# First attention of a two-layer block: the softmax weights are turned unscaled, and the scale is applied to the weighed output

## Chip, cores and metric

The kernel runs on one core of a Trainium2 chip. The metric is the device time of one execution in microseconds (us), median over several runs.

## What is computed

Two transformer-like blocks run one after the other on 512 tokens of width 1024, all in fp32. The first has, side by side, a neighbourhood attention with 8 heads of 64 and a two-directional state-space layer (SSD) with 8 heads of 64; their outputs are joined, go through `w_out`, and a gated feed-forward follows. The second block is a windowed attention and another feed-forward. The change lies in the first attention alone. Cut to its core, the reference says, for each grid row of 64 queries:

```python
s_loc = einsum("bwhd,brwkhd->bhwrk", q_r, k_win) * scale + bias     # 8 x 16 window
s_ctx = einsum("bwhd,bchd->bhwc", q_r, k_ctx) * scale               # 256 context keys
p = softmax(concatenate([s_loc, s_ctx], -1))
out = einsum(p_loc, v_win) + einsum(p_ctx, v_ctx)
```

## The kernel before

Weights stream in as 92 blocks of 128 x 2048. The large products take three passes in a rounded fp32 type: every operand x is held as a high part and a low part (x minus the high part), and TensorE (PE) adds high·high, high·low and low·high (`chunk_products`, L274). So every weight block and every activation needs a high part (a copy by ScalarE, ACT) and a low part (a subtraction by VectorE, DVE, or GpSimd, POOL). Semaphores are set by hand, and each engine runs its own program in the order in which it is written.

The first attention works on 16 groups (`NG = 16`), four query windows for each of four pairs of heads. A group G has two units, u = 2G and 2G + 1, one for each head of the pair, and a unit is 128 queries by 512 keys. The engines walk over turns. In turn G:

- PE (`attention1_pe`): `scores(G)` (L508, four products of 128 x 256 in all), `turn(G - 2)` for both units (L522, four 128 x 128 transposes each, into banks 1 and 2), `weigh(G - 3)` (L536, values times turned weights, two heads side by side on 64 output rows each, into bank 7 or 3). Scores have four banks.
- DVE (`attention1_dve`): `top` for both units (L601 and L603: bias added, and the row's extreme found), `inverse(G - 1)` (L610: reciprocal of the two row sums), `out_low(G - 4)` (L615: low half of the output, read from the bank). In turns 7, 9, 11 and 13 also a quarter of the low half of weight block 13 (L634).
- ACT (`attention1_act`): `exp` for both units (L562, it also sums the rows), `copy(G - 1)` for both units (L572, turned weights from the bank to SBUF), `out_high(G - 2)` (L578). The high half of weight block 13 (L258) stands between turns 3 and 4.
- POOL (`attention1_pool`): for each unit, the unscaled weights times the reciprocal of their row sum (L648), ahead of the turn; and after units 9, 13, 17 and 21 a quarter of the low half of weight block 12 (L656).

Turn 0 and turn 1 lie between the last projection products (tiles 22 and 23 of the input projection). Right behind the attention stands the SSD. Its first part is a chain of ten steps: POOL makes scaled inputs (L941), PE multiplies them (L968), DVE adds the product to the carried state (L1104 for the first two, then L1099 and L1102). POOL's step n waits for PE's step n - 2, PE's step n for DVE's step n - 2. Then PE makes masked sums (`sums`, L977 and L985), ACT the decay factors (L1069, L1073), and so on.

Of the kernel before, what the change touches and what calls it, by code (L numbers as in the profile page):

```python
# [6 lines left out]
ALU = mybir.AluOpType  # L7
# [90 lines left out]
def build(nc, T):  # L98

    es = ExitStack()  # L100
    with es:
# [98 lines left out]
        at1 = {n: sem(f"att1_{n}") for n in ("scores", "top", "nmax", "probs", "rinv", "norm", "ptr", "pt", "pv", "ohi", "olo")}  # L200
# [292 lines left out]
        prob1, pt1 = [A(at, 512) for at in A_PROB], [A(at, 4, 256) for at in A_PT]  # L493

        def attention1_pe(pe, turns):
# [29 lines left out]
            def weigh(G):  # L525
                j, t = G // 4, G % 4
                pe.wait_ge(s["pt"], 2 * G + 2)
                if G >= 2:
                    pe.wait_ge(s["olo"], G - 1)
                elif G == 1:  # L530
                    pe.wait_ge(tile_free, 24)
                for kb in range(4):
                    for odd in range(2):
                        head, half = slice(128 * j + 64 * odd, 128 * j + 64 * odd + 64), slice(128 * odd, 128 * odd + 128)
                        v = vkey[:, 2 * t + kb, head] if kb < 2 else vctx[:, kb - 2, head]
                        last = nc.tensor.matmul(ps[WEIGH1[G % 2]][64 * odd:64 * odd + 64, 0:128], v, pt1[G % 2][:, kb, half],  # L536
                                                start=kb == 0, stop=kb == 3)
                last.then_inc(s["pv"], 1)
# [10 lines left out]
        def out1(G):  # L549
            j, t = G // 4, G % 4  # L550
            hi, lo = (h[:, j:j + 1, :].rearrange("p a (r t c) -> p (a t) r c", r=ROWS, t=4)[:, t] for h in (h_hi, h_lo))
            return hi, lo, ps[WEIGH1[G % 2]][:, 0:128].rearrange("p (r c) -> p r c", r=ROWS)

        def attention1_act(act, turns):
# [20 lines left out]
            def out_high(G):  # L575
                act.wait_ge(s["pv"], G + 1)
                hi, lo, src = out1(G)
                nc.scalar.activation(hi, src, ACT.Copy).then_inc(s["ohi"], 1)  # L578

            for G in turns:  # L580
# [9 lines left out]
                if G >= 2:  # L590
                    out_high(G - 2)

        def attention1_dve(dve, turns):
# [18 lines left out]
            def out_low(G):  # L612
                dve.wait_ge(s["ohi"], G + 1)
                hi, lo, src = out1(G)
                nc.vector.tensor_tensor(lo, src, hi, ALU.subtract).then_inc(s["olo"], 1)  # L615

            for G in turns:
                if G == 2:
                    inverse(1)
# [3 lines left out]
                if G == 1:  # L623
                    inverse(0)
                if 3 <= G < NG + 1:
                    inverse(G - 1)
                if G in (7, 9, 11, 13):
                    q = (G - 7) // 2
                    if q == 0:
                        dve.wait_ge(hi_done, B_OUT + 2)  # L630
                    if q == 3:
                        dve.wait_ge(lo_done, B_OUT + 1)
                    part = slice(q * 512, q * 512 + 512)
                    last = nc.vector.tensor_tensor(w_lo[1][:, part], w_raw[1][:, part], w_hi[1][:, part], ALU.subtract)  # L634
                    if q == 3:
                        last.then_inc(lo_done, 1)
                if G >= 4:
                    out_low(G - 4)
# [5 lines left out]
        def attention1_pool(pool):  # L644
            s = at1
            for u in range(2 * NG):
                pool.wait_ge(s["rinv"], u // 2 + 1)
                nc.gpsimd.tensor_scalar(prob1[u % 4], prob1[u % 4], row_inv[:, u % 16:u % 16 + 1], 1.0,  # L648
                                        ALU.mult, ALU.mult).then_inc(s["norm"], 1)
                if u in (9, 13, 17, 21):  # L650
                    q = (u - 9) // 4
                    if q == 0:
                        pool.wait_ge(hi_done, B_OUT + 1)
                        pool.wait_ge(half_used, 2 * (B_OUT - 1))
                    part = slice(q * 512, q * 512 + 512)
                    last = nc.gpsimd.tensor_tensor(w_lo[0][:, part], w_raw[0][:, part], w_hi[0][:, part], ALU.subtract)  # L656
                    if q == 3:
                        last.then_inc(lo_done, 1)

# [431 lines left out]
        def ssd_dve(dve, link):  # L1091
            for n in range(10):
                d, k, c = n % 2, n // 2, ORDER[n % 2][n // 2]
                new = state0[:, d, :] if k == 0 else hin[:, 4 * d + AFTER[d][k], :]
                if k:
# [3 lines left out]
                    link(nc.vector.tensor_tensor(heads(new), heads(old), dec, ALU.mult))  # L1099
                dve.wait_ge(sd["st"], n + 1)  # L1100
# [575 lines left out]
        def _(act):  # L1676
# [110 lines left out]
            attention1_act(act, range(4, NG + 2))  # L1787
# [699 lines left out]
```

## Time and profile before

| | |
|---|---|
| median of 3 runs | 1347.22 us (1346.64 to 1348.71) |
| the profiled execution | 1348.49 us, of which the profile's span is 1346.7 us |
| PE matmul busy | 1292.5 us (96%) |
| DVE, ACT, POOL busy | 550.3, 569.1 and 594.8 us |
| granted PE clock, mean | 0.988 |
| the attention, from turn 2's first turned unit to the end of the last weighing | 245 to 297.6 us |

The profile's line numbers are those of the kernel before. In a timeline, one line is a run of equal instructions: its start, its length, and in brackets how long the engine had been idle and what ended that. An fp32 product takes two PE instructions, so `scores` counts 8, the transposes of a group 8, and `weigh` 16.

### The profile page before, as it was taken

Reading aid. Unit: us, or ns where it says so; the run is one execution under the profiler, and the core shown is the slowest. Engines: PE = TensorE matmul, PEld = TensorE weight load, DVE = VectorE, ACT = ScalarE, POOL = GpSimd, SP = SyncE. Lnnn points to the kernel's source line nnn. Section 1 sums busy time; section 2 is a strip of 40 time slices with the busy share of each in tenths; the row PEclk is TensorE's granted clock in tenths of the full one; section 3 lists DMA queues with packets and bytes.
Section 4 is the critical chain, followed back from the end, with each engine's and each line's share of the span. In section 5 each row is a group of like instructions: output and inputs, shape, how many; then the busy total and the mean of one; then the engine's idle time right before and its main releaser. Section 6 shows DMA issues by size and latency. Waiting matters only on the chain.

```text
span 1346.7 us, 17535 instructions
## 1 busy us (share of the span) xinstructions
PE 1292.5 (96%) x6464; PEld 1037.7 (77%) x6464; DVE 550.3 (41%) x1080; ACT 569.1 (42%) x938; POOL 594.8 (44%) x494
## 2 busy tenths in 40 slices
PE   8999999898989999999999899999899999999998
PEld 1788888676877888888888778667688888888886
DVE  2577652678436444443542362783520000001123
ACT  3712454777335333222323364785452323223232
POOL 0335232367235444444665642455224444445561
PEclk9899999999989999999999999999999999999999
DMA  9417547050233555554422312111202233222221
GB/s 393 177 75 272 186 167 146 1 188 1 68 152 130 208 195 196 198 195 156 156 94 94 141 63 94 56 29 62 92 32 94 96 102 106 101 93 94 94 93 63
DMA packets 27401, 166.76 MB, mean 124 GB/s; under 512 B 2976, under 2 KB 5280, under 8 KB 8656
## 3 DMA queue, kind: packets, MB, share of 16 engines
q1 hardware_dynamic: 25328, 151.31, 32.2%
q10 hardware_dynamic: 2016, 14.68, 2.9%
q8 instruction: 37, 0.61, 0.2%
q14 instruction: 20, 0.16, 0.0%
HBM read 163.85 MB, written 6.32 MB: 126 GB/s over the span
## 4 chain that ended last, share of the span: by engine, by line
PE 83%; DVE 7%; ACT 4%; DMA 3%; POOL 1%; issue 1%; SPq 0%; DVEq 0%; ACTq 0%
PE bank L274 54%; PE bank L333 12%; PE bank L310 6%; DMA ada_ring<-ada_dram 2%; DVE ada_ring L2005 1%; PE bank L1346 1%; PE bank L1318 1%; DMA w_raw<-w_dram 1%; PE bank L522 1%; PE bank L713 1%; DVE arena L2070 1%; PE bank L536 1%; PE bank L508 1%; POOL arena L941 1%; PE bank L702 1%
## 5 line engine op out<-in xcount | busy, mean ns | idle before, releaser
L267 POOL TENSOR_TENSOR w_lo<-w_raw,w_hi 128x512 fp32r<-128x512 f32 x336 | 457.8, 1393 | 615.8 <-ACT w_hi L258 615.8
L274 PE MATMUL bank<-h_hi,w_hi 128*128 128x512 f32 x1120 | 442.7, 395 | 9.6 <-DVE h_lo L449 6.6
L274 PE MATMUL bank<-h_lo,w_hi 128*128 128x512 f32 x1120 | 438.8, 392 | 0.0
L274 PE MATMUL bank<-h_hi,w_lo 128*128 128x512 f32 x1120 | 438.6, 392 | 0.0
L258 ACT ACTIVATE w_hi<-w_raw 128x2048 fp32r<-128x2048 f32 x88 | 168.6, 1916 | 306.5 <-PE bank L274 187.8
L274 PEld LDWEIGHTS bank<-h_hi,w_hi 128*128 128x128 f32 x1120 | 212.3, 190 | 57.0 <-issue 6.3
L274 PEld LDWEIGHTS bank<-h_hi,w_lo 128*128 128x128 f32 x1120 | 212.0, 189 | 44.6
L274 PEld LDWEIGHTS bank<-h_lo,w_hi 128*128 128x128 f32 x1120 | 212.4, 190 | 42.6
L2342 DVE TENSOR_TENSOR arena<-arena,bank 128x512 f32 (+1 forms) x22 | 15.1, 688 | 210.2 <-PE bank L274 210.2
L2198 DVE TENSOR_TENSOR h_lo<-arena,h_hi 128x1024 fp32r<-128x1024 f32 x22 | 32.4, 1486 | 135.1 <-ACT h_hi L1822 123.6
L2024 DVE SCALAR_TENSOR_TENSOR arena<-bank,params,arena 128x511 f32<-128x511 f32 (+1 forms) x36 | 25.4, 705 | 130.0 <-ACT arena L1797 109.7
L333 PE MATMUL bank<-w_hi,h_hi 128*128 128x512 f32 x176 | 68.7, 390 | 0.0
L333 PE MATMUL bank<-w_lo,h_hi 128*128 128x512 f32 x176 | 68.5, 389 | 0.0
L333 PE MATMUL bank<-w_hi,h_lo 128*128 128x512 f32 x176 | 68.5, 389 | 0.0
L2015 DVE CUSTOM_DVE_ANT_0 ada_ring<-ada_ring,arena 128x1024 f32<-128x1024 f32 x48 | 62.3, 1334 | 0.0
L2005 DVE CUSTOM_DVE_ANT_0 ada_ring<-ada_ring,arena,params 128x1024 f32<-128x1024 f32 x32 | 48.1, 1545 | 10.6 <-DMA ada_ring<-ada_dram 10.4
L898 POOL TENSOR_SCALAR arena<-arena,small 128x256 f32<-128x256 f32 (+1 forms) x64 | 33.2, 532 | 36.4 <-DVE small L839 36.4
L1797 ACT ACTIVATE arena<-bank,params 128x512 f32<-128x512 f32 x22 | 17.1, 779 | 70.4 <-PE bank L274 70.4
L310 PE MATMUL bank<-h_hi,w_hi 128*128 128x512 f32 x112 | 43.7, 390 | 0.0
L310 PE MATMUL bank<-h_hi,w_lo 128*128 128x512 f32 x112 | 43.6, 389 | 0.0
L310 PE MATMUL bank<-h_lo,w_hi 128*128 128x512 f32 x112 | 43.6, 389 | 0.0
L1346 PE MATMUL bank<-arena_rounded,w_hi 128*128 128x256 f32 x224 | 40.4, 282 | 2.7 <-DVE arena L2026 1.8
(274 smaller groups left out, 1714.4 us busy)
## 6 DMA issues: line engine op xcount, KB each, us to landing
w_raw<-w_dram SPq DMA_DIRECT2D x92, 1024.0 KB, 4.8
ada_ring<-ada_dram SPq DMA_DIRECT2D x30, 1024.0 KB, 4.8
ada_ring<-ada_dram ACTq DMA_DIRECT2D x14, 1024.0 KB, 4.9
arena<-ada_dram SPq DMA_DIRECT2D x4, 1024.0 KB, 10.7
arena<-x_dram SPq DMA_DIRECT2D x2, 2048.0 KB, 11.5
bias_copies<-bias_rows SPq DMA_DIRECT2D x1, 4096.0 KB, 17.4
arena<-bias_copies SPq DMA_DIRECT2D x4, 768.0 KB, 5.8
ada_ring<-rpb_dram SPq DMA_DIRECT2D x16, 128.0 KB, 9.4
```

The costliest lines, as they stand in the source:

```text
L258: nc.scalar.activation(w_hi[b % 2][:], w_raw[b % 2][:], ACT.Copy).then_inc(hi_done, 1)
L267: last = nc.gpsimd.tensor_tensor(w_lo[b % 2][:, part], w_raw[b % 2][:, part], w_hi[b % 2][:, part], ALU.subtract)
L274: last = nc.tensor.matmul(bank[:, :], w[:, ft, k, :], x[:, k, :], start=k == first and m == 0, stop=k == final and m == 2)
L310: last = nc.tensor.matmul(ps[f][:, :], w[:, k, f, :], x[:, 2 * gslot + k, :], start=bank_free is not None and k == 0 and m == 0, stop=False)
L333: last = nc.tensor.matmul(ps[2 * t + h][:, :], x[:, slot + k, part], w[n][:, k, cols], start=start and m == 0, stop=stop and m == 2)
L898: nc.gpsimd.tensor_scalar(prob2[:, u % 8, 0:w], prob2[:, u % 8, 0:w], row_inv[:, u % 16:u % 16 + 1], 1.0, ALU.mult, ALU.mult).then_inc(s[" ...
L1346: last = nc.tensor.matmul(ps[4 + n % 2][:, 0:CTX], w[:, n % 2, k, :], x[:, k, :], start=k == 0 and m == 0, stop=k == DC - 1 and m == 2)
L1797: nc.scalar.activation(buf, bank[:, :], ACT.Identity, bias=fconv[:, 3, bass.ds(j, 1)], scale=fconv[:, 1, bass.ds(j, 1)]).then_inc(tap_done, 1)
L2005: last = nc.vector.tensor_tensor_reduce(out=src, in0=src, in1=row1, scale=1.0, scalar=par_("adab")[:, 16 + at:17 + at], op0=ALU.mult, op1= ...
L2015: last = nc.vector.tensor_tensor_reduce(out=src, in0=src, in1=row2, scale=1.0, scalar=0.0, op0=ALU.mult, op1=ALU.add, accum_out=dots[:, 2 ...
L2024: link(nc.vector.scalar_tensor_tensor(out=buf[:, 1:n], in0=src[:, 0:n - 1], scalar=w[:, 0, m], in1=buf[:, 1:n], op0=ALU.mult, op1=ALU.add))
L2198: nc.vector.tensor_tensor(h_lo[:, slot:slot + 2, :], HID[:, chunk, :], h_hi[:, slot:slot + 2, :], ALU.subtract)\
```

## The change

The weights are no longer scaled ahead of the turn. `turn` waits for the exponentials (`probs`) alone, and POOL's 32 scalings (L648) and their semaphore go. In their place `weigh(G)` first makes two products on PE: the column of reciprocals of each unit, repeated over 64 stationary columns, times the identity, which puts each query's reciprocal into columns 128 to 256 of the output bank, beside the weighed output. DVE (`out_scale`) copies these 128 columns to SBUF, and multiplies the output of the bank by them into one of two SBUF buffers. ACT's `out_high` reads that buffer, two turns later than before, and POOL now makes the low half (`out1_low`), from SBUF. DVE's `inverse` moves by a turn (`inverse(G - 2)` in turn G). POOL takes the low halves of both weight blocks 12 and 13, a quarter ahead of each `out1_low` of groups 1 to 8; DVE's L634 goes. The last two `out1_low`, of groups 14 and 15, stand in the SSD's first POOL loop, ahead of its step 4.

```diff
             def turn(G, odd):
                 u = 2 * G + odd
-                pe.wait_ge(s["norm"], u + 1)
+                pe.wait_ge(s["probs"], u + 1)
...
                 pe.wait_ge(s["pt"], 2 * G + 2)
                 if G >= 2:
-                    pe.wait_ge(s["olo"], G - 1)
+                    pe.wait_ge(s["scaled"], G - 1)
...
+                pe.wait_ge(s["rinv"], G + 1)
+                for odd in range(2):
+                    col = (2 * G + odd) % 16
+                    nc.tensor.matmul(ps[WEIGH1[G % 2]][64 * odd:64 * odd + 64, 128:256], row_inv[:, col:col + 1].to_broadcast([P, 64]), ident,
+                                     start=True, stop=True)
...
+        def out1_low(G):
+            nc.gpsimd.wait_ge(at1["ohi"], G + 1)
+            hi, lo, src = out1(G)
+            nc.gpsimd.tensor_tensor(lo, src, hi, ALU.subtract).then_inc(at1["olo"], 1)
...
             def out_high(G):
-                act.wait_ge(s["pv"], G + 1)
+                act.wait_ge(s["scaled"], G + 1)
...
-                if G >= 2:
-                    out_high(G - 2)
+                if G >= 4:
+                    out_high(G - 4)
...
+            def out_scale(G):
+                dve.wait_ge(s["pv"], G + 1)
+                nc.vector.tensor_copy(inv_spread[:, G % 2, :], ps[WEIGH1[G % 2]][:, 128:256]).then_inc(s["spread"], 1)
+                if G >= 2:
+                    dve.wait_ge(s["olo"], G - 1)
+                dve.wait_ge(s["spread"], G + 1)
+                nc.vector.tensor_tensor(out_scaled[G % 2], ps[WEIGH1[G % 2]][:, 0:128], inv_spread[:, G % 2, :], ALU.mult).then_inc(s["scaled"], 1)
...
         def attention1_pool(pool):
...
-                nc.gpsimd.tensor_scalar(prob1[u % 4], prob1[u % 4], row_inv[:, u % 16:u % 16 + 1], 1.0,
-                                        ALU.mult, ALU.mult).then_inc(s["norm"], 1)
...
+            for G in range(NG - 2):
+                if 1 <= G < 9:
+                    b, q = (G - 1) // 4, (G - 1) % 4
...
+                    last = nc.gpsimd.tensor_tensor(w_lo[b][:, part], w_raw[b][:, part], w_hi[b][:, part], ALU.subtract)
...
+                out1_low(G)
...
             for n in range(10):
                 d, c = n % 2, ORDER[n % 2][n // 2]
+                if n == 4:
+                    for G in (NG - 2, NG - 1):
+                                out1_low(G)
```

In the change the lines have other numbers: the transposes are L523, the spreading products L536, the weighing L542, `out1_low` L563, and the SSD's first POOL loop L942. PE's program at the end of the attention stood so before (turns 15 to 18, then the SSD's L968):

```order
L508 MATMUL bank<-arena 128x256 x4
L522 MATMUL bank<-constants,arena 128x128 x8
L536 MATMUL bank<-arena 64x128 x8
L522 MATMUL bank<-constants,arena 128x128 x8
L536 MATMUL bank<-arena 64x128 x8
L522 MATMUL bank<-constants,arena 128x128 x8
L536 MATMUL bank<-arena 64x128 x16
L968 MATMUL bank<-arena 128x256 x20
```

and now (turns 16 to 18):

```order
L523 MATMUL bank<-constants,arena 128x128 x8
L536 MATMUL bank<-constants,small 64x128 x2
L542 MATMUL bank<-arena 64x128 x8
L523 MATMUL bank<-constants,arena 128x128 x8
L536 MATMUL bank<-constants,small 64x128 x2
L542 MATMUL bank<-arena 64x128 x8
L536 MATMUL bank<-constants,small 64x128 x2
L542 MATMUL bank<-arena 64x128 x8
L969 MATMUL bank<-arena 128x256 x20
```

Each weighing has two more products ahead of it, and nothing else moved on PE. POOL's program from the attention into the SSD stood so before:

```order
L656 TENSOR_TENSOR w_lo<-w_raw,w_hi 128x512
L648 TENSOR_SCALAR arena<-arena,small 128x512 [waits att1_rinv] x10
L941 TENSOR_TENSOR arena<-arena,small 128x512 [waits ssd_wend]
L941 TENSOR_TENSOR arena<-arena,small 128x512
L941 TENSOR_TENSOR arena<-arena,small 128x512 [waits ssd_st] x8
```

and now (the `out1_low` of groups 12 to 15 and the ten L942; `small` and `w_dt` are the two buffers of the scaled output):

```order
L563 TENSOR_TENSOR h_lo<-small,h_hi 128x8x16 [waits att1_ohi]
L563 TENSOR_TENSOR h_lo<-w_dt,h_hi 128x8x16 [waits att1_ohi]
L942 TENSOR_TENSOR arena<-arena,small 128x512 [waits ssd_wend]
L942 TENSOR_TENSOR arena<-arena,small 128x512
L942 TENSOR_TENSOR arena<-arena,small 128x512 [waits ssd_st] x2
L563 TENSOR_TENSOR h_lo<-small,h_hi 128x8x16 [waits att1_ohi]
L563 TENSOR_TENSOR h_lo<-w_dt,h_hi 128x8x16 [waits att1_ohi]
L942 TENSOR_TENSOR arena<-arena,small 128x512 [waits ssd_st] x6
```

POOL's first SSD step now stands behind a wait for ACT's high half of group 13, and two low halves stand between its steps 3 and 4.

## Rows read from the trace of the kernel before

**Rows 1.** The page: busy time of PE, and the chain that ended last
```profile
PE 1292.5 (96%) x6464; PEld 1037.7 (77%) x6464; DVE 550.3 (41%) x1080; ACT 569.1 (42%) x938; POOL 594.8 (44%) x494
...
PE 83%; DVE 7%; ACT 4%; DMA 3%; POOL 1%; issue 1%; SPq 0%; DVEq 0%; ACTq 0%
```

**Rows 2.** Busy time of each engine in 245 to 298 us
```profile
245.00:298.00 53.00, 49.33 (x490) 36.54 (x491) 36.99 (x126) 42.78 (x108) 30.75 (x38) 1.00 0.28 97
```

**Rows 3.** Waits in 245 to 298 us: total us, times, longest
```profile
PE bank L522 <- POOL arena L648: 4.5, 4, 1.8
```

**Rows 4.** Chain that ended last: start, us, what
```profile
262.41 1.06 PE bank L508 x8
263.47 1.02 PE bank L522 x8
264.49 1.02 PE bank L536 x16
...
301.22 8.44 POOL arena L941 x6
...
311.55 2.19 ACT ada_ring L1069 x8
```

**Rows 5.** Timeline of turns 7, 8, 9 and 15 to the SSD: start us, us, engine, what
```profile
262.34 1.13 PE L508 MATMUL bank<-arena 64*128 64x256 f32 x8
...
265.45 1.13 PE L508 MATMUL bank<-arena 64*128 64x256 f32 x8
...
266.60 1.32 PE L522 MATMUL bank<-constants,arena 128*128 128x128 f32 x8
...
268.87 1.13 PE L508 MATMUL bank<-arena 64*128 64x256 f32 x8
...
288.48 1.14 PE L508 MATMUL bank<-arena 64*128 64x256 f32 x8
...
292.39 1.32 PE L522 MATMUL bank<-constants,arena 128*128 128x128 f32 x8 [0.72 <-POOL arena L648]
...
297.58 1.99 PE L968 MATMUL bank<-arena 128*128 128x256 f32 x8
```

**Rows 6.** Nearest rows for the new operations: groups by shape, one timeline line, one line's durations
```profile
L898 POOL TENSOR_SCALAR arena<-arena,small 128x256 f32<-128x256 f32 x32 | 14.9, 478 | 15.4 <-DVE small L839 15.4
...
355.10 1.05 PE L1055 MATMUL bank<-constants,small 128*128 128x128 f32 x8
...
L941 POOL TENSOR_TENSOR arena<-arena,small x10: 1037/1483/2026, 294.9 to 308.2; 128x512 f32<-128x512 f32 x10
...
L2105 DVE COPY y_squares<-small x2: 220/223/226, 202.8 to 203.0; 128x128 f32<-128x128 f32 x2
```

**Rows 7.** Timeline of turns 2 to 6, where the loop fills
```profile
247.95 0.69 DVE L2080 TENSOR_TENSOR arena<-arena 128x512 f32<-128x512 f32 x1
...
251.84 1.13 PE L508 MATMUL bank<-arena 64*128 64x256 f32 x8
...
255.78 1.90 ACT L258 ACTIVATE w_hi<-w_raw 128x2048 fp32r<-128x2048 f32 x1
...
259.07 1.13 PE L508 MATMUL bank<-arena 64*128 64x256 f32 x8 [0.40 <-ACT arena L562]
```

**Rows 8.** Timeline of the last turns and the SSD's first steps, in order of time
```profile
294.66 1.09 PE L522 MATMUL bank<-constants,arena 128*128 128x128 f32 x8
...
294.95 3.03 POOL L941 TENSOR_TENSOR arena<-arena,small 128x512 f32<-128x512 f32 x2
...
295.30 1.77 DVE L641 TENSOR_TENSOR arena_rounded<-y_squares,constants 128x1024 fp32r<-128x1024 f32 x1
295.36 1.09 ACT L572 ACTIVATE arena<-bank 128x512 f32<-128x512 f32 x2 [0.30 <-PE bank L522]
...
296.83 0.28 ACT L578 ACTIVATE h_hi<-bank 128x128 fp32r<-128x128 f32 x1 [0.38 <-PE bank L536]
...
298.80 2.16 POOL L941 TENSOR_TENSOR arena<-arena,small 128x512 f32<-128x512 f32 x2 [0.83 <-PE bank L968]
```

More of the change, by code:

```diff
@@ L199, in build @@
             "add_left", "add_right", "x_left", "x_right", "x_bias", "x_root", "x_inv", "xn_left", "xn_right"))
-        at1 = {n: sem(f"att1_{n}") for n in ("scores", "top", "nmax", "probs", "rinv", "norm", "ptr", "pt", "pv", "ohi", "olo")}
+        at1 = {n: sem(f"att1_{n}") for n in ("scores", "top", "nmax", "probs", "rinv", "ptr", "pt", "pv", "spread", "scaled", "ohi", "olo")}
         at2 = {n: sem(f"att2_{n}") for n in ("scores", "nmax", "probs", "sinkin", "sinke", "rinv", "norm",
@@ L493, in build @@
         prob1, pt1 = [A(at, 512) for at in A_PROB], [A(at, 4, 256) for at in A_PT]
+        out_scaled, inv_spread = [small[:, 384:512], wdt[:, :]], A(A_STATE + 512, 2, 128)
         def attention1_pe(pe, turns):
@@ L551, in out1 @@
             hi, lo = (h[:, j:j + 1, :].rearrange("p a (r t c) -> p (a t) r c", r=ROWS, t=4)[:, t] for h in (h_hi, h_lo))
-            return hi, lo, ps[WEIGH1[G % 2]][:, 0:128].rearrange("p (r c) -> p r c", r=ROWS)
+            return hi, lo, out_scaled[G % 2].rearrange("p (r c) -> p r c", r=ROWS)
+        def out1_low(G):
+            nc.gpsimd.wait_ge(at1["ohi"], G + 1)
+            hi, lo, src = out1(G)
+            nc.gpsimd.tensor_tensor(lo, src, hi, ALU.subtract).then_inc(at1["olo"], 1)
         def attention1_act(act, turns):
@@ L610, in inverse @@
                 nc.vector.reciprocal(row_inv[:, two], row_sum[:, two]).then_inc(s["rinv"], 1)
[L612 to L615, printed above, removed]
+            def out_scale(G):
[5 more added lines that the diff above has]
+                nc.vector.tensor_tensor(out_scaled[G % 2], ps[WEIGH1[G % 2]][:, 0:128], inv_spread[:, G % 2, :], ALU.mult).then_inc(s["scaled"], 1)
             for G in turns:
-                if G == 2:
-                    inverse(1)
                 if G < NG:
@@ L622, in attention1_dve @@
                     top(G, 1)
[L623 to L636, printed above, removed]
+                if 2 <= G < NG + 2:
+                    inverse(G - 2)
                 if G >= 4:
-                    out_low(G - 4)
+                    out_scale(G - 4)
                 if G in (NG + 1, NG + 2):
@@ L644, in attention1_pool @@
         def attention1_pool(pool):
-            s = at1
-            for u in range(2 * NG):
-                pool.wait_ge(s["rinv"], u // 2 + 1)
-                nc.gpsimd.tensor_scalar(prob1[u % 4], prob1[u % 4], row_inv[:, u % 16:u % 16 + 1], 1.0,
-                                        ALU.mult, ALU.mult).then_inc(s["norm"], 1)
-                if u in (9, 13, 17, 21):
-                    q = (u - 9) // 4
+            for G in range(NG - 2):
+                if 1 <= G < 9:
+                    b, q = (G - 1) // 4, (G - 1) % 4
                     if q == 0:
-                        pool.wait_ge(hi_done, B_OUT + 1)
+                        pool.wait_ge(hi_done, B_OUT + 1 + b)
+                    if G == 1:
                         pool.wait_ge(half_used, 2 * (B_OUT - 1))
                     part = slice(q * 512, q * 512 + 512)
-                    last = nc.gpsimd.tensor_tensor(w_lo[0][:, part], w_raw[0][:, part], w_hi[0][:, part], ALU.subtract)
+                    last = nc.gpsimd.tensor_tensor(w_lo[b][:, part], w_raw[b][:, part], w_hi[b][:, part], ALU.subtract)
                     if q == 3:
                         last.then_inc(lo_done, 1)
+                out1_low(G)
         NG = 16
@@ L1099, in ssd_dve @@
                     link(nc.vector.tensor_tensor(heads(new), heads(old), dec, ALU.mult))
+                if n == 1:
+                    dve.wait_ge(at1["scaled"], NG)
                 dve.wait_ge(sd["st"], n + 1)
@@ L1786, in _ @@
             high(act, B_OUT + 1)
-            attention1_act(act, range(4, NG + 2))
+            attention1_act(act, range(4, NG + 4))
             ssd_act(act)
```

## Prediction

> **What bounds the kernel now.** I read the page first. PE is busy for 96% of the span, and the chain that ended last is PE for 83% [rows 1]: time is lost or won where PE waits or gets more work. So the place of the change has to be looked at for PE alone. From 245 to 298 us PE is busy for 49.3 of 53 us, ACT for 42.8, DVE for 37.0 and POOL for 30.8 [rows 2]. The waits of that stretch say what is missing: PE's transposes waited 4.5 us in four longer waits for POOL's scaling [rows 3]. That wait is what the change takes away. What is it worth, and what do the added products cost?
>
> The chain gives the length of PE's parts when nothing holds them: scores 1.06 us, the eight transposes 1.02, the weighing's 16 instructions 1.02 [rows 4], so a turn takes 3.10. The timeline agrees for turn 7, whose scores start at 262.34 and those of turn 8 at 265.45. Turn 8 takes 3.42, to 268.87, since its transposes are spread over 1.32 instead of some 1.06: POOL was late by 0.3 us [rows 5]. This pair repeats: the scores of turn 15 start at 288.48, eight turns after turn 7, so a turn takes 3.27 on average. The loop is thus bound by PE's own work, with 0.16 us of waiting a turn.
>
> **The added products.** Each weighing gets two fp32 products of 64 output rows by 128 columns, four PE instructions of the form that L536 has (there the two heads go side by side on 64 output rows each, and here too). 16 of these take 1.02 us [rows 4], so one takes 0.064 and four take 0.26. From above: if the pair did not overlap, each instruction would cost what a full-width one of the same kind costs, a repeated column times the identity, 1.05 / 8 = 0.131 [rows 6], so 0.52 for four. From below: nothing, if they slip into time that PE loses anyway between parts. I take 0.26, since L536 has their shape and their neighbours. A turn then takes 3.10 + 0.26 = 3.36, against 3.27 before: **the products cost 0.1 us a turn more than the removed wait gives.**
>
> **PE, turn by turn.** The first turned units may now start at once behind the scores of turn 2, but this gives nothing: copying them out waits for DVE's L2080, which ends at 248.6 [rows 7] and does not move, and DVE's next four row maxima, 0.87 us each, follow. I get the scores of turn 4 at 251.8, as before (251.84). From there nothing holds PE. Turn 4 gains what its transposes waited for POOL. In turn 6 the scores waited for ACT, 0.40 us, because the high half of weight block 13, 1.9 us, stood ahead of the exponentials [rows 7]. ACT now starts it some 0.8 us earlier, since no high half of an output, with its wait for the weighing, is in front of it any more, and ends the exponentials by 258.3. PE wants them at 251.8 + 2 x 3.36 = 258.5, so this wait goes too. The scores of turn 15 start at 251.8 + 11 x 3.36 = 288.8, where 288.48 was. Turn 15 ends at 292.1. Turns 16 and 17 have no scores: 2.30 each, without the 0.72 us that turn 16 waited for POOL at 292.39 [rows 5]. They end at 296.7, and the last weighing, 1.28, at 298.0. Before, the SSD's first product started at 297.58 [rows 5]. Net so far: **+0.4 us.**
>
> **The other engines in the loop.** ACT has the same work. Its high halves read SBUF two turns later, when they are ready, so it no longer waits for PE there: 2.7 us of work in 3.36. DVE loses L615 and its quarter subtractions, and gets a copy of 128 columns, some 0.22 us [rows 6], and a multiplication like L615: with 37.0 of 53 us busy, or 2.3 of 3.3 a turn [rows 2], it stays under 2.7 a turn. POOL has 1.3 us for a quarter and one small subtraction a turn. `scaled` and `rinv`, for which PE's weighing now waits, are made in the DVE turn before. I cost all of this at nothing. The cover is 0.6 us a turn on DVE and ACT; if it were gone, each 0.1 us of it would cost 1.4 us. The SP queue's loads of blocks 14 and 15 wait for the low halves; these are done no later than before.
>
> **POOL's small subtraction.** The trace has none of 128 columns. It reads 2 x 128 elements, as the scaling of 256 columns does, 0.48 us [rows 6]. Below: a quarter of the fastest L941 of 512 columns, 1.04 / 4 = 0.26. Above: 0.48 times the slowdown of a typical L941 against the fastest, 1.48 / 1.04 [rows 6], 0.68. I take 0.48. The Trainium skill (GPSIMD Engine Reference, section 3.1) has 4497 ns for this operation on 2048 columns, against 2293 on the vector engine, and so speaks against moving it; an estimate from it in proportion is 0.28, and the sum below would be +1.4 instead of +2.0.
>
> **The end, where POOL is on the path.** Behind the attention the chain is POOL's: L941 back to back for 8.44 us from 301.22 [rows 4]. Before, POOL made the first two steps from 294.95, 3.03 us, while PE was still weighing; step 2 then waited for PE and started at 298.80 [rows 8]. Now POOL may start step 0 only behind the low half of group 13, and this behind ACT's high half. The last transposes start at 294.4; the copies start 0.70 later (295.36 behind 294.66), take 1.1 to 296.2, then come two high halves, 0.28 each [rows 8], to 296.75, and the low half with its semaphore, 0.55: POOL starts step 0 at 297.3 instead of 294.95. Two steps take 3.03 beside DVE's L641 and 2.16 without [rows 8]; L641 is beside about half of them, so 2.7. The fast and the slow price differ, I think, because DVE's L641 and L1099 read two SBUF operands. The Trainium skill (GPSIMD Engine Reference, section 8) says that POOL shares its SBUF interfaces with such DVE instructions; by it the slow price would hold for just as long as L641 runs, and if that were all of both steps the sum would be +2.3. Step 2 starts at 300.0, 1.2 later than before. Steps 2 and 3 took 2.42 before, of which 0.27 a wait for PE; now 2.2, and then two low halves, 0.96, stand in front of step 4: 303.2 instead of 301.22. **So +2.0 us, which contains the 0.4.** Steps 4 to 9, the sums and ACT's decay factors from 311.55 on [rows 4] are one chain behind it and move by the same 2.0; later PE is full, nothing gives it back.
>
> **The sum.** The profiled execution would go from 1348.5 to 1350.5. It is 1.3 above the median of the runs; against the median, 1347.2 + 2.0 = **1349.2 us**. A measurement of this kernel tells about 0.2% from no change, 2.7 us, so this is within "same", near its edge. The forecast's own range, with the bounds of the three low halves on the path (-0.7 to +0.6) and of the two POOL steps (-0.5 to +0.3), is 1348.0 to 1350.2.
>
> **The rivals.**
> 1. *The two spreading products do not overlap* (0.52 instead of 0.26 in 15 weighings, from turn 4 on). PE's own work decides, so all of it counts: +3.9 more, 1353.1, slower. For it: only an order of one head's two instructions, then the other's, and a stationary operand that is one column repeated, which no row has at 64 columns. Against it: L536 has the same order and costs 0.064. It turns the sign of the verdict as soon as four instructions take over 0.30 us. Chance 0.15.
> 2. *POOL stays longer on the path*: POOL beside DVE is slowed in all its steps, or an `out1_low` is as dear as 0.68 and the loop's last ones queue up. Up to 1351.3. Chance 0.12.
> 3. *The products are hidden*: they cost next to nothing, a turn takes 3.10, and -3.9 stands against the +2.0: 1345.3. This is the other sign. The point from which it decides is 0.13 us for four instructions. For it: PE's instructions overlap at their ends, a 128-column one lasts 0.27 in the trace and takes 0.13. Against it: the chain already counts the overlapped time. Chance 0.10.
> 4. *The removed wait comes back as another*: PE waits for the exponentials or for `scaled`. By the times above the exponentials are over 2 us early, and `scaled` 1.8. Then 1350 to 1353, or in turns with luck no loss; with all that I don't see, chance 0.08.
>
> **How the numbers follow.** The forecast has 0.55: 0.42 within 0.2% and 0.13 above. Rival 1 is slower (0.15), rival 2 mostly (0.08 of 0.12), rival 3 is 0.07 same and 0.03 faster, the rest 0.04 faster, 0.02 and 0.02. That makes faster 0.07, same 0.55, slower 0.38. The range reaches to rivals 3 and 1: 1345.3 to 1353.1; what lies outside is part of the rest.
>
> **What would show it.** Right: no wait of PE's transposes for POOL, turns of 3.36 us, all alike, and the SSD's first product at about 298. POOL's step 0 at 297.3, its step 4 at 303.2, with two operations of about half a microsecond ahead of it; ACT's first decay factors at 313.5. Wrong: turns of 3.6 (rival 1) or 3.1 (rival 3), a wait of PE for ACT or DVE inside the turns, or a first SSD step of POOL before 296.

## The result: 0.4% slower, where 0.15% was forecast

| | kernel before | changed kernel |
|---|---|---|
| median of 5 runs each | 1347.49 us | 1353.99 us |
| lowest to highest | 1346.64 to 1348.71 | 1352.21 to 1354.70 |
| the profiled execution: its time, its span | 1348.5, 1346.7 us | 1354.5, 1352.7 us |
| mean granted clock of TensorE | 0.988 | 0.984 |

The ratio of the runs is 1.0041, with the interval 1.003 to 1.0052: some 5.5 us slower (the medians lie 6.5 apart), where 2.0 were forecast and the prediction counted 2.7 (0.2%) as a difference. The median lies 0.9 us above the top of the range. In a second comparison the changed kernel took 1352.68 us, ratio 1.0034 (1.0022 to 1.0046).

### The profile after

First the page: its head, the busy times and the row of the granted clock (a digit is a fortieth of the span, 33.8 us).

```profile
span 1352.7 us, 17679 instructions
PE 1299.6 (96%) x6528; PEld 1045.3 (77%) x6528; DVE 550.6 (41%) x1092; ACT 567.6 (42%) x938; POOL 581.0 (43%) x482
PEclk9999999899999999999999999999989999999999
```

It answers to [rows 1] and says little: PE is the bound as before. The waits of 245 to 305 us (total us, times, longest) say more:

```profile
POOL h_lo L563 <- ACT h_hi L589: 57.5, 13, 35.7
PE bank L523 <- ACT arena L583: 2.9, 1, 2.9
```

The waits of the transposes for POOL [rows 3] are gone, as the change meant. What is new is one single wait of 2.91 us, behind the early turned units of group 0. Two of the four waits of [rows 3] lay at the same place before, in turns 2 and 3:

```profile
245.38 1.32 PE L522 MATMUL bank<-constants,arena 128*128 128x128 f32 x8 [1.77 <-POOL arena L648]
249.56 1.33 PE L522 MATMUL bank<-constants,arena 128*128 128x128 f32 x8 [1.79 <-POOL arena L648]
```

They are 3.56 of the 4.5 us. The timeline of PE after shows what stands there now, 0.74 and 2.91, together 3.65 us of waiting for ACT, and what follows (start, us, engine, line, what, count, in brackets the idle time before the group and what ended it):

```profile
244.76 1.13 PE L509 MATMUL bank<-arena 64*128 64x256 f32 x8 [0.74 <-ACT arena L573]
248.81 1.94 PE L523 MATMUL bank<-constants,arena 128*128 128x128 f32 x8 [2.91 <-ACT arena L583]
250.68 0.70 PE L536 MATMUL bank<-constants,small 128*64 128x128 f32 x4
251.16 1.92 PE L542 MATMUL bank<-arena 128*64 128x128 f32 x16
253.01 1.73 PE L509 MATMUL bank<-arena 64*128 64x256 f32 x8
254.67 1.09 PE L523 MATMUL bank<-constants,arena 128*128 128x128 f32 x8
255.69 0.44 PE L536 MATMUL bank<-constants,small 128*64 128x128 f32 x4
255.96 1.04 PE L542 MATMUL bank<-arena 128*64 128x128 f32 x16
256.93 1.14 PE L509 MATMUL bank<-arena 64*128 64x256 f32 x8
```

The same eight transposes take 1.94 us at 248.81 and 1.09 at 254.67, the 16 weighing instructions 1.92 and then 1.04. Nothing of their shape has changed; the clock has. The windows of these stretches (from and to, us, then busy us and instructions of PE, its weight loads, DVE, ACT, POOL, then granted clock, DMA share, GB/s):

```profile
244.00:255.00 11.00, 7.35 (x48) 5.75 (x48) 7.65 (x21) 5.57 (x14) 0.00 (x0) 0.69 0.01 1
248.80:254.70 5.90, 5.89 (x37) 4.73 (x37) 2.78 (x13) 4.12 (x11) 0.00 (x0) 0.54 0.01 3
308.00:310.00 2.00, 1.68 (x6) 1.39 (x6) 1.71 (x3) 0.00 (x0) 1.29 (x3) 0.72 0.00 0
310.00:313.00 3.00, 3.00 (x9) 2.08 (x9) 2.85 (x4) 0.00 (x0) 2.11 (x3) 0.62 0.00 0
```

From 248.8 to 254.7 PE was granted 0.54 of full speed, nearly all of it at 1.2 GHz instead of 2.4; over 244 to 255 the mean is 0.69, where the kernel before had 1.00. The two last rows, 0.72 and 0.62, lie behind the idle piece of 1.64 us that PE has in the SSD, before 306.87.

From 255 us on the chain that ended last shows the loop as forecast (start, us, what; ten turns alike):

```profile
257.00 1.06 PE bank L509 x8
258.07 1.02 PE bank L523 x8
259.09 0.37 PE bank L536 x4
259.46 0.87 PE bank L542 x16
260.33 1.06 PE bank L509 x8
...
297.88 0.87 POOL h_lo L563 x2
298.76 2.99 POOL arena L942 x2
...
304.05 1.28 POOL h_lo L563 x2
```

A turn is 3.33 us. Spreading and weighing together take 0.37 + 0.87 = 1.24, where the weighing took 1.02 [rows 4]: the four spreading instructions cost 0.22 us. Behind the loop two pairs of low halves (L563) stand on the chain, where the forecast had one low half and one pair: the low half of group 12 has queued up ahead of that of group 13.

### Where the 6.0 us of span are

The stretches begin at R, ACT's first copy of turned scores (248.73 before, 248.06 after), and end at the starts of five events: the scores of turns 5 and 15, POOL's SSD steps 0 and 4, and ACT's first decay factors.

| stretch, us | before | forecast | after |
|---|---|---|---|
| R to the scores of turn 5 | 6.76 | 6.4 | **8.87** |
| ten turns | 32.99 | 33.6 | 33.30 |
| scores of turn 15 to POOL's step 0 | 6.47 | 8.5 | 8.48 |
| step 0 to step 4 | 6.27 | 5.9 | 6.58 |
| step 4 to the decay factors | 10.33 | 10.3 | 10.78 |
| sum | 62.82 | 64.8 | 68.01 |

The sum is 5.2 us longer. R itself comes 0.7 earlier, which is scatter of what lies before: in the other profiles, of the experiments too, it lies between 246.4 and 248.6. So the decay factors are 4.5 us later (316.07 against 311.55). The second profiles of both kernels (a_again, b_again) show the same size: from R to the decay factors 67.36 us against 62.85. The remaining 1.5 of 6.0 arise in 355 to 370 us, in a stretch of weight products that the change does not touch; see the end of the experiments.

### The profile page after: what moved, and what is told of

It is laid out like the page before. It is cut to its first block, busy times and chain, and to the rows that moved or that the text cites. A ratio compares the mean times of both kernels' runs of the same rounds, so it can differ in the third digit from the quotient of the medians.

```text
span 1352.7 us, 17679 instructions
## 1 busy us (share of the span) xinstructions
PE 1299.6 (96%) x6528; PEld 1045.3 (77%) x6528; DVE 550.6 (41%) x1092; ACT 567.6 (42%) x938; POOL 581.0 (43%) x482
## 4 chain that ended last, share of the span: by engine, by line
PE 83%; DVE 7%; ACT 5%; DMA 3%; POOL 1%; issue 1%; SPq 0%; ACTq 0%; DVEq 0%
PE bank L274 53%; PE bank L333 12%; PE bank L310 6%; DMA ada_ring<-ada_dram 2%; DVE ada_ring L2008 1%; PE bank L1321 1%; PE bank L523 1%; PE bank L509 1%; PE bank L1349 1%; DVE arena L2073 1%; DMA w_raw<-w_dram 1%; PE bank L542 1%; PE bank L711 1%; ACT arena L759 1%; DVE bank L824 1%
```

## The experiments

Twelve runs, in three batches; each ratio is to the kernel before in the same batch. The changed kernel itself was run in the second batch only. The theory was that the long idle piece ahead of 248.81 lowers the clock (some 2.3 us) and that POOL's low halves on the way into the SSD cost the rest. The rivals were that the spreading products cost more than the trace's 0.22, and that the whole is due to something outside the attention.

### Fill the idle piece: x1_fill

Twenty transposes without use go behind the scores of turn 3, into a corner of a bank that is free then.

```diff
                     scores(G)
+                if G == 3:
+                    for _ in range(20):
+                        nc.tensor.transpose(ps[WEIGH1[0]][:, 384:512], con_("trif"), ident)
```

> The changed kernel with 20 dummy transposes (2.6 us of PE work into unused columns of bank 7) behind the scores of turn 3, where PE stood idle for 2.9 us until 248.81 and the granted clock was 0.54 in the 5.9 us behind it. Theory A (the idle piece of 2.9 us, made by the early turn of group 0, brings the low clock): the granted clock stays 1.00 from 249 to 255, the scores of turn 5 start at about 255.1 instead of 256.93, and the time is 1.8 us lower, about 1352.2. Rival (the clock fell there for another reason, or the low clock hides behind DVE's waits): the clock falls again, or the scores of turn 5 stay at 256.9, and the time is the same, 1354.0.

Measured: 1351.08 us, ratio 1.0022 (1.0012 to 1.0031). PE has more work and the kernel is no slower for it; the interval just touches that of the changed kernel's first comparison and overlaps that of its second, so the profile decides. The window and the timeline of PE:

```profile
244.00:255.00 11.00, 9.55 (x97) 7.68 (x95) 9.90 (x30) 7.43 (x19) 0.00 (x0) 1.00 0.01 1
```

```profile
249.31 1.12 PE L523 MATMUL bank<-constants,arena 128*128 128x128 f32 x8 [0.58 <-ACT arena L586]
251.79 1.13 PE L509 MATMUL bank<-arena 64*128 64x256 f32 x8
```

The clock is 1.00, the transposes take 1.12 instead of 1.94, and R to the scores of turn 5 is 6.55 us instead of 8.87: 2.3 us. With the clock up, the events are within 0.4 us of the forecast: scores of turn 4 at 251.79 (forecast 251.8), of turn 15 at 288.42 (288.8), POOL's step 0 at 296.91 (297.3), step 4 at 303.47 (303.2). Behind the SSD's idle piece of 1.64 us the clock fell here too, to 0.60 over 306 to 310 us, and the decay factors come 11.08 us behind step 4.

### Avoid the idle piece: x6_late

The turned units of group 0 are made behind the scores of turn 3, as they were before the change. Everything else stays changed.

```diff
-                if 2 <= G < NG + 2:
+                if G == 3:
+                    turn(0, 0)
+                    turn(0, 1)
+                if 3 <= G < NG + 2:
                     turn(G - 2, 0)
```

> The changed kernel, but the transposes of group 0 stand behind the scores of turn 3, where PE comes to them about as late as in the kernel before: the same idle time ahead of the first copies, in two pieces of about 1.8 and 1.3 us instead of 0.7 and 2.9, and no work added. Theory A (it is the one long idle piece that brings the low clock): the clock stays 1.00 until turn 5, the time falls by 1.5 to 2.5 us against the changed kernel. Rival (the sum of idle time decides, or filling it was what helped): the clock falls as before and the time is that of the changed kernel.

Measured: 1351.42 us, ratio 1.0020 (1.0012 to 1.0029). PE now waits twice, in pieces of 1.77 and 1.88 us:

```profile
243.15 1.14 PE L509 MATMUL bank<-arena 64*128 64x256 f32 x8 [1.77 <-ACT arena L576]
...
247.19 1.12 PE L523 MATMUL bank<-constants,arena 128*128 128x128 f32 x8 [1.88 <-ACT arena L586]
```

Together that is 3.65 us, as in the changed kernel, so not the sum of the idle time decides but its division. The clock over 244 to 255 is 1.00. R to turn 5 is again 6.55. The sum from R to the decay factors is 65.13, 2.3 more than before: that is the change without the clock, forecast as 2.0. Fill and late order agree, by two different means, that the early turn cost up to 2.3 us and gave nothing.

### Spreading products, none and twice: x3_nospread, x4_twice

In x3 the two products are dropped from each weighing, so the output is multiplied by whatever stands in those columns of the bank:

```diff
-                for odd in range(2):
-                    col = (2 * G + odd) % 16
-                    nc.tensor.matmul(ps[WEIGH1[G % 2]][64 * odd:64 * odd + 64, 128:256], row_inv[:, col:col + 1].to_broadcast([P, 64]), ident,
-                                     start=True, stop=True)
```

> The changed kernel without the two spreading products of each group (this part of the computation is left out: the output is multiplied by what stands in the bank's columns 128 to 256). Theory (PE's own work bounds the loop): a turn takes 3.10 instead of 3.33 us, 15 weighings from turn 4 on give 3.4 us back, about 1350.5. Rival (another engine or a latency is close behind PE): a turn stays above 3.2, and less than half comes back, 1352.3 or more.

In x4 the same lines stand twice.

> The changed kernel with both spreading products made twice. Theory (PE's own work bounds the loop, and a pair of products costs 0.23 us): a turn takes 3.56 us, the time rises by 3.4 us to about 1357.4. Rival 1 of the prediction in weaker form (the pair is dearer when the two heads do not overlap with neighbours): a turn takes 3.6 to 3.85 us, 1358 to 1362.

Measured: 1348.97 us (1.0006, 0.9997 to 1.0015) and 1355.66 us (1.0058, 1.0044 to 1.0071). The timelines of PE, first x3, then x4, one turn each:

```profile
270.98 1.14 PE L509 MATMUL bank<-arena 64*128 64x256 f32 x8
...
274.10 1.13 PE L509 MATMUL bank<-arena 64*128 64x256 f32 x8
```

```profile
270.75 1.13 PE L509 MATMUL bank<-arena 64*128 64x256 f32 x8
...
272.84 0.44 PE L536 MATMUL bank<-constants,small 128*64 128x128 f32 x4
273.11 0.39 PE L540 MATMUL bank<-constants,small 128*64 128x128 f32 x4
...
274.30 1.14 PE L509 MATMUL bank<-arena 64*128 64x256 f32 x8
```

Turns take 3.11, 3.33 and 3.55 us with none, one and two pairs. The price is 0.22 a pair, on a straight line: neither hidden (rival 3) nor 0.52 (rival 1). Both times are lower than expected (1350.5 and 1357.4, worked out from the changed kernel's first comparison). Both profiles still have the idle piece of 2.9 us, and both a clock of 0.84 over 244 to 255, where that first comparison's profile has 0.69.

### POOL's low halves: x2_tail, x8_tail2

x2 gives DVE the low halves of groups 13 to 15, the last two ahead of its own SSD steps 0 and 1.

```diff
         def out1_low(G):
-            nc.gpsimd.wait_ge(at1["ohi"], G + 1)
+            eng = nc.gpsimd if G < NG - 3 else nc.vector
+            eng.wait_ge(at1["ohi"], G + 1)
...
+                if n < 2:
+                    out1_low(NG - 2 + n)
                 dve.wait_ge(sd["st"], n + 1)
...
```

> The changed kernel with the low halves of groups 13, 14 and 15 made by DVE instead of POOL: POOL's first SSD step no longer waits for group 13, and nothing stands ahead of its step 4. Theory (POOL is the path there): step 0 starts 0.4 us earlier, steps 3 to 4 lose the 0.90 and 0.45 us of the two low halves, together 1.5 to 1.8 us: about 1352.3. Rival (DVE's own steps or the clock of PE set the pace there, so POOL's time comes back as another wait): under 0.5 us, 1353.5 to 1354.

Measured: 1350.85 us, ratio 1.0020 (1.001 to 1.0029); its clock over 244 to 255 was 0.84. POOL's step 0 starts 8.06 us behind the scores of turn 15 instead of 8.48 and step 4 comes 6.16 later instead of 6.58. Of these 0.8 us, 0.5 reach PE's last step: it starts 22.94 us behind the scores of turn 15, against 23.44 in x6, whose low halves lie as in the changed kernel and whose clock stayed up there. In between PE now waits for DVE:

```profile
300.95 1.10 PE L969 MATMUL bank<-arena 128*128 128x256 f32 x4 [0.76 <-DVE arena L1109]
```

x8 leaves all low halves with POOL, but puts them where it would wait anyway: 12 and 13 between its SSD steps 0 and 1, 14 and 15 in its next loop, behind the second scaling there (L950), where its next operation waits for DVE. PE waits for them later, ahead of the product that reads them.

```diff
-                if n == 4:
-                    for G in (NG - 2, NG - 1):
-                                out1_low(G)
+                if n == 1:
+                    out1_low(NG - 4)
+                    out1_low(NG - 3)
...
                 nc.gpsimd.tensor_tensor(heads(x_dt[n % 4]), heads(xtok[:, c, :]), dtc, ALU.mult).then_inc(sd["m"], 1)
+                if n == 1:
+                    out1_low(NG - 2)
+                    out1_low(NG - 1)
...
```

> The changed kernel with POOL's low halves moved off its path: SSD step 0 ahead of the low halves of groups 12 and 13, those of groups 14 and 15 behind the ten steps where POOL waits for DVE, and PE's sums wait for DVE's scaling instead of the low halves. Theory (POOL is the path there): step 2 starts 1.2 to 1.4 us earlier after the last turn, step 4 another 1.3 us earlier; of these 2.6 us some comes back as DVE's pace, as in the run with the low halves on DVE, so 1.0 to 2.5 us less than the changed kernel. Rival (DVE's ten steps are the bound anyway): under 0.5 us.

Measured: 1350.18 us, ratio 1.0016 (1.0007 to 1.0025). The timeline of POOL:

```profile
294.54 1.04 POOL L942 TENSOR_TENSOR arena<-arena,small 128x512 f32<-128x512 f32 x1
296.15 0.83 POOL L563 TENSOR_TENSOR h_lo<-small,h_hi 128x128 fp32r<-128x128 f32 x1 [0.57 <-ACT h_hi L589]
296.94 0.45 POOL L563 TENSOR_TENSOR h_lo<-w_dt,h_hi 128x128 fp32r<-128x128 f32 x1
297.37 3.02 POOL L942 TENSOR_TENSOR arena<-arena,small 128x512 f32<-128x512 f32 x2
300.65 9.73 POOL L942 TENSOR_TENSOR arena<-arena,small 128x512 f32<-128x512 f32 x7 [0.27 <-PE bank L972]
```

Step 0 starts 6.04 us behind the scores of turn 15 (8.48 after, 6.47 before), and steps 3 to 9 run through without a low half among them. PE's last step starts 21.9 us behind the scores of turn 15, against 23.4 in x6: 1.5 us come from the place of the low halves. (x8 keeps the early turn, and its clock over 244 to 255 is 0.84.)

### All repairs, and none of the products: x10_all_late, x11_none

x10 is x6 and x8 together. x11 is x10 without the spreading products, so with the full removal of the wait and none of its price.

> The changed kernel with both repairs: the transposes of group 0 behind the scores of turn 3, and POOL's low halves off its path in the SSD. The sum: turns of 3.33 instead of 3.27 on average cost about 0.9 us against the kernel before; the repairs take 2.3 us of low clock and 1.5 us of POOL's 2.4 away. From the first copy to ACT's first decay factors 63.5 to 64.5 us (62.8 before, 68.0 changed), time 1.000 to 1.0015 of before. Rival (there is a further cost of the change that no run has shown): above 1.002.

> The same with both repairs, and without the spreading products (this part of the computation is left out). By the sum 15 x 0.22 = 3.3 us less than with them: 60.2 to 61.2 us from the first copy to the decay factors, 0.9975 to 0.999 of before. Rival (part of the products' cost lies beside something else): over 62 us, 1.000.

Measured: x10 1347.69 us, ratio 0.9994 (0.9984 to 1.0003); x11 1347.15 us, ratio 0.9988 (0.9979 to 0.9997). From R to the decay factors x10 takes 63.65 us and x11 61.04, against 62.82 before and 68.01 after. So by the times the mended change equals the kernel before, and by its profile it is 0.8 us longer: of the 5.2 us, 4.4 are the two avoidable costs. What the products cost more than the removed wait is in part made up by POOL's better order. Even with the spreading for nothing, the profile is 1.8 us (0.13%) shorter than before, no more.

### Remove the wait without products: x7_bpool

The prediction took 0.16 us of waiting a turn from [rows 5]: in turns 8, 10, 12 and 14 the transposes came some 0.3 us late. In these turns POOL scaled beside DVE's quarter of weight block 13 (before; then the two scalings a turn later, without it):

```profile
265.31 0.67 DVE L634 TENSOR_TENSOR w_lo<-w_raw,w_hi 128x512 fp32r<-128x512 f32 x1
265.49 1.72 POOL L648 TENSOR_SCALAR arena<-arena,small 128x512 f32<-128x512 f32 x2 [1.90 <-DVE small L610]
...
268.61 1.36 POOL L648 TENSOR_SCALAR arena<-arena,small 128x512 f32<-128x512 f32 x2 [0.16 <-DVE small L610]
```

x7 is the kernel before, with all quarters on POOL, one behind each of eight groups, and none left to DVE.

```diff
-                if G in (7, 9, 11, 13):
-                    q = (G - 7) // 2
...
-                    last = nc.vector.tensor_tensor(w_lo[1][:, part], w_raw[1][:, part], w_hi[1][:, part], ALU.subtract)
...
-                if u in (9, 13, 17, 21):
-                    q = (u - 9) // 4
+                if u % 2 and 9 <= u < 25:
+                    b, q = (u - 9) // 8, (u - 9) // 2 % 4
...
```

> The kernel before, in which POOL makes the low halves of both weight blocks (a quarter behind every group from unit 9 to 23) and DVE none. Theory (in turns 8, 10, 12 and 14 PE waits because DVE's quarter in the turn before slows POOL's scaling from 1.36 to 1.71 us for two): these four turns take 3.1 instead of 3.4 us, 1.3 us less, about 0.999 of before. Rival (the wait comes from POOL's own latency behind the reciprocals): the same time.

Measured: 1346.72 us, ratio 0.9989 (0.998 to 0.9997). The timeline of PE has turns of 3.11 us from turn 7 to turn 15, with no wait for POOL inside:

```profile
262.16 1.14 PE L508 MATMUL bank<-arena 64*128 64x256 f32 x8
...
265.28 1.13 PE L508 MATMUL bank<-arena 64*128 64x256 f32 x8
```

So this wait of [rows 5] goes once DVE's quarter no longer stands beside POOL's scaling, although POOL has four quarters more to make, and PE gets no work for it. POOL's two scalings take 1.36 us in every turn. From the scores of turn 5 to those of turn 15 it is 31.75 us against 32.99: 1.2 us. The waits in turns 2, 3 and 16, which make up most of [rows 3], stay (1.77, 1.24 and 0.72 us).

### The two kernels again: a_again, b_again, x7_again

The changed kernel, the kernel before and x7, each as a kernel under test.

> The changed kernel once more, beside the next three on the same chip. The sum as it now stands: 2.3 us for a low granted clock in turns 3 and 4, behind PE's idle piece of 2.9 us, 2.4 us until POOL's SSD step 4 (0.9 from longer turns, the rest from POOL's later first step and its two low halves), and a remainder of 0 to 1.5 us. 1353.0 to 1354.5, ratio to before 1.004. Theory A also expects the clock under 0.8 in turns 3 and 4 again; if it fell there by chance, it should be 1.00 in some profiles of this program.

> The kernel before once more, for its profile: does the granted clock fall between 244 and 255 us there too, as it did in the profile of the version with all low halves on POOL, which has the same order on PE up to turn 4? Theory A in its strong form (only the 2.9 us idle piece does it): 1.00. In its weak form (the fall is a matter of chance, and the long idle piece makes it likely): 0.67 to 1.00. Time: ratio 1.000 within 0.001.

> The kernel before with the low halves of both weight blocks on POOL, a second time, to narrow its interval. Theory: 1.3 us faster than before, 0.9985 to 0.9995; turns of 3.11 us from turn 7 to 15. Rival (the first result was chance): 1.000.

Measured: the changed kernel 1352.68 us, 1.0034 (1.0022 to 1.0046); the kernel before, against itself, 1347.10, 0.9993 (0.9984 to 1.0001); x7 1347.48, also 0.9993 (0.9984 to 1.0002). The kernel compared with itself comes out as far below 1 as x7 does, so x7's gain is seen in its profiles, but the times do not confirm it. The same holds for x11. In the profile of a_again the clock over 244 to 255 was 0.84, not under 0.8 as expected; in that of b_again 1.00, which leaves both forms of the theory open.

### What the profiles say of the clock together

| kernels | idle pieces of PE before 249 | clock over 244 to 255 us |
|---|---|---|
| changed, a_again, x2, x3, x4, x8 | 0.74, then one of 2.9 | 0.69, 0.84, 0.84, 0.84, 0.84, 0.84 |
| x1 (filled) | 0.75 and 0.58 | 1.00 |
| x6, x10, x11 (late order) | 1.77 and 1.9 | 1.00 in all three |
| before, b_again, x7, x7_again | 1.77, then 1.79, 1.79, 1.24, 0.39 | 1.00, 1.00, 0.69, 0.86 |

The low clock came with the long piece six times in six, and without it twice in eight. In the changed kernel's first profile it had fallen to 0.50 already within the piece, over 248 to 249 us; in a_again it fell behind it. So the long piece makes the low clock likely, and it is not the only cause: in both profiles of x7 the clock fell behind the first piece of 1.77 us, which before and b_again have as well, at 1.00. What decides there stays open.

The price differs as well. At full clock the changed order takes 6.55 us from R to the scores of turn 5 (x1, x6). The profile with 0.69 took 2.3 us more, those of a_again, x2 and x8 with 0.84 took 1.1 to 1.4 more. And it depends on what follows: in x7_again the clock was 0.50 from 243.7 to 247.1, in work that ended in a wait anyway. The second wait shrank to 0.39 us, and R to turn 5 took 6.77, as before (6.76). In x7, where the low clock reached into the dense work behind, it took 7.99.

The idle piece of 1.64 us in the SSD is in six profiles. In three the clock fell behind it, and POOL's step 4 to the decay factors took 10.78, 11.09 and 11.08 us (after, a_again, x1); in three it stayed at 1.00, and the stretch took 10.22 (x3, x4, x6). (In x3 it had fallen earlier, to 0.50 over 298 to 300, behind another idle piece of 2.17 us.) Where the low halves lie elsewhere (x2, x8, x10, x11) the piece is gone and the clock there was 1.00.

**The remaining 1.5 us.** In 355 to 370 us the clock was 0.89 in the profile after and 1.00 before, and on the chain one group of weight products reads:

```profile
362.93 7.37 PE bank L274 x24
```

Before it took 5.74. Of the other profiles x1, x2, x4, x6, x7, x7_again, x8 and x11 show the 0.89, x3, x10, a_again and b_again the 1.00, so both kinds come with and without the change's parts. It is part of the difference of two profiled executions and not, as far as these runs show, of the change. No run was made for it.

## Why the prediction was wrong, by its own steps

**"The first turned units may now start at once …, but this gives nothing."** Here it failed. The copying does wait for DVE, as said, and the scores of turn 4 do not come earlier. But I looked only at what the early units gain, not at what they leave: before, PE waited twice, 1.77 and 1.79 us, with transposes and scores between; once these are moved ahead PE has nothing for 2.91 us in one piece. The granted clock was then 0.54 for 5.9 us of dense work. Missing term: 2.3 us in the first profile (8.87 against 6.55 in both x1 and x6), 1.4 in the second (7.92). No rival held it either. Nor is most of the wait of [rows 3] taken away: its 3.56 us of turns 2 and 3 came back as 3.65 of waiting for ACT. TensorE: Matmul & The Clock Gate in the Trainium skill, section Loop structure matters more than you think, warns of a long wait between matmuls, there for a DMA, after which they run cold. The trace agrees for this one wait for ACT, with 1.94 against 1.09 us for the same eight transposes. The same page (Part 1) says that the number of slow matmuls at a kernel's start varies between runs of one kernel; inside this kernel the means of 0.69 and 0.84 vary too.

**The added products, 0.26 us.** Right in kind, 0.22 measured; a turn is 3.33 instead of 3.36. From turn 5 on PE has no wait in the loop, neither for ACT nor for DVE: what was costed at nothing cost nothing.

**The first POOL step at 297.3, step 4 at 303.2.** Near: 296.91 and 303.47 in x1, where the clock stayed up till then, but in part by luck. Between the last copies and step 0 the forecast had 1.1 us, of two high halves and one low half; the trace has the same 1.1, of which two low halves take 0.83, the first starting 0.27 behind the copies. From step 0 to step 4 it measures 6.58 where 5.9 was forecast, and this term was sized too small. POOL's first two steps take 3.0 instead of 2.7: L641 was taken to slow POOL for as long as both run, while the second step is held until L641 ends (see the last section). The sum of +2.3, with the slow price for both steps, had this right in size. The small subtraction was put at 0.48 and takes 0.46 alone; held by DVE it took 0.90, beyond the upper bound of 0.68, which came from the slowdown of a typical L941. That is 0.3 more. The ten turns, 0.3 shorter than forecast, hide half of it.

**"Steps 4 to 9 … move by the same 2.0."** Nearly. POOL, held by two low halves (1.28 us), leaves PE idle for 1.64 us before 306.87; the clock is 0.72 and 0.62 in the windows behind it, and the stretch takes 10.78 instead of 10.33 us. In x3 and x6, with the same idle piece and no low clock, PE's last step starts 8.38 us behind step 4; in the changed kernel it is 8.94. Second missing term, of the same kind: 0.6 us (0.9 in a_again), where the clock falls, which it did in three profiles of six.

**The sum.** With the clock up, x6 measures +2.3 us from R to the decay factors where +2.0 was forecast; the two clock terms (2.3 and 0.6) make +5.2 of it. By the times the late order gives back 1.9 to 2.8 us (1.0020 against 1.0034 and 1.0041), with intervals that overlap in the first case; that the profile and the times agree carries this more than the times alone. The rest of the excess lies in the stretch of 355 to 370 us and in the scatter.

**The rivals and the chances.** Rival 1's time, 1353.1, is near the measured 1353.99, but its mechanism is not what happened. Rival 2 came true in kind: a low half took 0.90 and the loop's last ones queued up, but that is under 1 us (its 1351.3 has no working). "Slower" had 0.38, all of it from the spreading products, from POOL, from a new wait or from the forecast's own scatter, none from the clock; the forecast's own range ended at 1350.2.

## To carry to other kernels

A wait that is taken away with work on the engine that bounds the kernel is worth only the difference of the two: here 0.16 us of waiting against 0.22 of products a turn, and taking the DVE operation away that stood beside the helper's (x7) removed the same 0.16 without any work for PE. When work of TensorE moves ahead of a wait, read how long an idle piece it leaves behind and what dense stretch comes next; if nothing is gained by being early, leave it late. Small operations put on a helper engine cost nothing only until that engine is itself on the path; look for the last of them, and put those where the engine would wait.

## What the hardware showed unexpectedly

- Adding 20 idle transposes to PE made the kernel some 1.6 us faster by the ratios of the second comparison (1.0022 against 1.0034) and 2.6 by the first (1.0041); in its profile the stretch from R to turn 5 is 2.3 us shorter. The times alone do not settle it, since its interval overlaps that of the second comparison.
- A POOL operation that starts while DVE is busy with two SBUF operands does not run slower: it is held until DVE's operation ends. From the timelines of POOL and DVE after, in order of time:

```profile
298.71 1.04 POOL L942 TENSOR_TENSOR arena<-arena,small 128x512 f32<-128x512 f32 x1
298.82 2.02 DVE L641 TENSOR_TENSOR arena_rounded<-y_squares,constants 128x1024 fp32r<-128x1024 f32 x1
299.71 2.02 POOL L942 TENSOR_TENSOR arena<-arena,small 128x512 f32<-128x512 f32 x1
...
303.64 0.96 DVE L1100 TENSOR_TENSOR arena<-arena,chunk_decay 128x512 f32<-128x512 f32 x1
304.00 0.90 POOL L563 TENSOR_TENSOR h_lo<-small,h_hi 128x128 fp32r<-128x128 f32 x1
304.63 0.69 DVE L1105 TENSOR_TENSOR arena<-arena,bank 128x512 f32<-128x512 f32 x1
304.87 0.45 POOL L563 TENSOR_TENSOR h_lo<-w_dt,h_hi 128x128 fp32r<-128x128 f32 x1
```

  The first SSD step starts before L641 and takes 1.04, as where DVE is idle, though L641 covers nearly all of it; L641 then takes 2.02, against 1.22 for the one at 296.56. The second step starts beside L641 and ends 0.90 behind its end. The first low half starts beside L1100 and ends 0.31 behind its end; the second lies beside L1105, which reads one SBUF operand and one bank, and takes 0.45, no more than alone. The low halves of 0.83 us in x8 and 1.27 in x11 fit this and no fixed factor: both end 0.31 to 0.32 behind the end of the DVE operation in whose time they start. The Trainium skill (GPSIMD Engine Reference, section 8) says that POOL shares its SBUF interfaces with VectorE and contends with DVE instructions that have two SBUF inputs; the trace agrees.
- A kernel compared with itself in the same batch gave 0.9993 (0.9984 to 1.0001): an effect of 0.1% needs the profile beside the times.
